# Moving the S4 weight sum of nine units by 192 bytes in a fused fp32 two-block kernel

## The reference, cut to what matters

```python
def swiglu_ffn(x, w_in, w_out):                      # first block, twice
    gate, up = jnp.split(x @ w_in, 2, axis=-1)       # 1024 x 5632
    return (jax.nn.silu(gate) * up) @ w_out

def conv_ffn(x, w_up, conv_w, conv_b, w_down):       # second block, twice
    up = x @ w_up                                    # 1024 x 5632
    a, g = up[..., :D_FF_2], up[..., D_FF_2:]
    g = causal_dwconv(g, conv_w) + conv_b
    return (jax.nn.gelu(g) * a) @ w_down

def mixer_c(x, w_in, conv_w, w_out):                 # second block, once
    proj = x @ w_in                                  # 1024 x 3072
    gate_b, gate_c, h = jnp.split(proj, 3, axis=-1)
    y = gate_b * causal_dwconv(gate_c * h, conv_w)
    return y @ w_out
```

## Time and profile before

| what | value |
|---|---|
| three timed executions | 2286.74, 2280.14, 2286.81 us; median 2286.74 |
| the profiled execution, its own time | 2293.73 us |
| its span in the trace | 2291.9 us |
| TensorE (PE) busy | 2274.3 us, 99% of the span, 15278 matmuls |
| weight loads (PEld) busy | 2081.8 us |
| VectorE, ScalarE, POOL busy | 1542.2, 1019.2, 354.9 us |
| HBM read | 234.46 MB, 103 GB/s over the span |
| mean granted clock of TensorE | 0.998 of full speed |

### The profile page before, as it was taken

One profiled execution on the slowest core, in us unless ns is written; L12 is line 12 of the kernel. 1 busy time (PEld: TensorE's weight loads), 2 busy tenths in 40 slices (PEclk: granted clock), 3 DMA queues, 4 the chain that ended last, 5 costly groups with the idle time before them and its releaser, 6 DMA issues.

```text
span 2291.9 us, 35530 instructions
## 1 busy us (share of the span) xinstructions
PE 2274.3 (99%) x15278; PEld 2081.8 (91%) x15278; DVE 1542.2 (67%) x1756; ACT 1019.2 (44%) x1283; POOL 354.9 (15%) x222
## 2 busy tenths in 40 slices
PE   9999999999999999999999999999999999999998
PEld 8999889897799998898988999988998988999987
DVE  7777436564587764356846999835886656999835
ACT  5555335455555543234333555522453442555521
POOL 2332000230133220001000322100230000322100
PEclk9999999999999999999999999999999999999999
DMA  4333323212133332242421333332233522232331
GB/s 171 111 111 111 110 74 139 74 52 78 37 113 109 111 111 102 74 173 90 168 90 37 129 105 112 112 115 77 108 100 124 200 74 74 93 108 99 129 109 55
DMA packets 34732, 238.83 MB, mean 104 GB/s; under 512 B 4108, under 2 KB 4492, under 8 KB 6800
## 3 DMA queue, kind: packets, MB, share of 16 engines
q1 hardware_dynamic: 34432, 236.56, 29.5%
q10 hardware_dynamic: 144, 0.00, 0.0%
HBM read 234.46 MB, written 2.10 MB: 103 GB/s over the span
## 4 chain that ended last, share of the span: by engine, by line
PE 96%; DVE 2%; DMA 1%; POOL 0%; ACT 0%; issue 0%; SPq 0%; DVEq 0%; POOLq 0%
PE bank L646 33%; PE bank L780 30%; PE bank L629 18%; PE bank L745 4%; PE bank L1132 4%; PE bank L768 1%; PE bank L986 1%; PE bank L1160 1%; PE bank L1181 1%; DVE w_lo L1871 1%; DMA raw<-w_full 1%; PE bank L918 0%; PE bank L928 0%; PE bank L825 0%; DVE s_lo L1987 0%
## 5 line engine op out<-in xcount | busy, mean ns | idle before, releaser
L1871 DVE TENSOR_TENSOR w_lo<-raw,w_hi 128x2048 fp32r<-128x2048 f32 (+1 forms) x207 | 475.1, 2296 | 362.5 <-ACT w_hi L1306 313.2
L1306 ACT ACTIVATE w_hi<-raw 128x2048 fp32r<-128x2048 f32 x207 | 395.1, 1909 | 326.0 <-DMA raw<-w_full 319.5
L780 PE MATMUL bank<-w_hi,h_hi 128*128 128x512 f32 x692 | 269.9, 390 | 0.0
L780 PE MATMUL bank<-w_hi,h_lo 128*128 128x512 f32 x692 | 269.4, 389 | 0.0
L780 PE MATMUL bank<-w_lo,h_hi 128*128 128x512 f32 x692 | 269.3, 389 | 0.0
L562 POOL TENSOR_TENSOR s_raw<-raw 128x512 f32<-128x512 f32 x84 | 115.7, 1378 | 545.0 <-PE bank L646 385.4
L646 PE MATMUL bank<-t_hi,s_hi 128*128 128x256 f32 x672 | 187.5, 279 | 3.2 <-ACT cc L1360 3.2
L646 PE MATMUL bank<-t_hi,w_hi 128*128 128x256 f32 x672 | 187.3, 279 | 3.0 <-DVE h L2023 3.0
L646 PE MATMUL bank<-u_hi,w_hi 128*128 128x256 f32 x672 | 187.5, 279 | 0.0
L646 PE MATMUL bank<-u_hi,w_lo 128*128 128x256 f32 x672 | 187.3, 279 | 0.0
L646 PE MATMUL bank<-u_lo,w_hi 128*128 128x256 f32 x672 | 187.2, 279 | 0.0
(11 more groups left out here) (386 smaller groups left out, 6096.9 us busy)
## 6 DMA issues: line engine op xcount, KB each, us to landing
raw<-w_full SPq DMA_DIRECT2D x207, 1024.0 KB, 4.9
rows_ab<-rows SPq DMA_DIRECT2D x8, 1024.0 KB, 7.0
x<-x SPq DMA_DIRECT2D x4, 512.0 KB, 4.5
mem_raw<-mem SPq DMA_DIRECT2D x2, 1024.0 KB, 9.0
out<-x SPq DMA_DIRECT2D x3, 512.0 KB, 2.6
raw<-w_full SPq DMA_DIRECT2D x2, 512.0 KB, 7.3
ab_rows<-ab_rows SPq DMA_DIRECT2D x1, 768.0 KB, 6.4
wg_raw<-w_gates SPq DMA_DIRECT2D x1, 512.0 KB, 7.2
```

What stands on the lines that cost most here:

```text
L780: done = mm(bank[:, 2 * t + n, :], act_in[:, k, tok(t)], w[:, s, c0:c0 + T], start=(first and r == 0 and j == 0), stop=(last and r == 1 an ...
L1306: S.activation(w_hi[:, u % SLOTS, :], raw[:, u % SLOTS, :], ACT.Copy).then_inc(w_hi_done, 1)
L1871: V.tensor_tensor(w_lo[:, u % SLOTS, at:FULL], raw[:, u % SLOTS, at:FULL], w_hi[:, u % SLOTS, at:FULL], ALU.subtract).then_inc(w_split, 1)
```

## The change

S4 gets three areas in place of two. Units with an even number take `even`, those with an odd number `odd`, both at place 0 as before; of the odd ones, the units whose distance from the run's first unit, halved and rounded down, leaves 2 when divided by 4 take `aligned`: raw and low parts at 100.6875 KB and the high part at 102.6875 KB, that is place 192, where B22 (the second 256 columns of the second half of `u`) stands. These are units 8 and 16 of runs 1 and 3, units 7 and 15 of runs 2 and 5, and unit 8 of run 4 (cin). `even` has its high part at 105 KB. Every engine's instructions stay the same in number, kind, shape and order; only addresses differ. In the changed file the lines below L130 stand 6 to 8 further down.

```diff
--- before.py
+++ after.py
@@ -126,9 +126,9 @@
         s23_raw = arena("s23_raw", [P, 2, 2 * QS], f32, 82.5)
         s23_lo = arena("s23_lo", [P, 2, 2 * QS], f32r, 82.5)
         s23_hi = arena("s23_hi", [P, 2, 2 * QS], f32r, 90.5)
-        s4_raw = arena("s4_raw", [P, 2, QS], f32, 98.5)
-        s4_lo = arena("s4_lo", [P, 2, QS], f32r, 98.5)
-        s4_hi = arena("s4_hi", [P, 2, QS], f32r, 102.5)
+        s4_place = {"even": (98.5, 105), "odd": (100.5, 102.5), "aligned": (100.6875, 102.6875)}
+        s4_whole, s4_low, s4_high = ({k: arena(f"s4_{n}_{k}", [P, QS], dt, at[i]) for k, at in s4_place.items()}
+                                     for n, dt, i in (("raw", f32, 0), ("lo", f32r, 0), ("hi", f32r, 1)))
 
         h_hi = arena("h_hi", [P, 2 * SLOTS, T], f32r, 50.5)
         h_lo = arena("h_lo", [P, 2 * SLOTS, T], f32r, 66.5)
@@ -376,6 +376,12 @@
         def lower_late(f, u):
 
             return ch_late[:, u % 2, :] if f == "c" else h32[:, u, 256:512]
+
+        def s4_kind(f, u):
+
+            if NTH_SEVEN[f, u] % 2 == 0:
+                return "even"
+            return "aligned" if (u - FIRST[f]) // 2 % 4 == 2 else "odd"
 
         def first_of_run(f, u):
             return not is_seven(f, u - 1)
@@ -554,7 +560,7 @@
             def rest_weight_sums(f, u):
 
                 j, w = NTH_SEVEN[f, u], raw[:, (U0[NAME[f]] + u) % SLOTS, :]
-                s2, s4 = s23_raw[:, j % 2, 0:QS], s4_raw[:, j % 2, :]
+                s2, s4 = s23_raw[:, j % 2, 0:QS], s4_whole[s4_kind(f, u)][:, :]
                 gp.wait_ge(first_sum, j + 1)
                 at = list(SEVENS[f]).index(u)
                 if at >= 2:
@@ -666,7 +672,7 @@
                 j, s, b = NTH_SEVEN[f, u], (U0[name] + u) % SLOTS, up_bank(f, u)
                 w = w_hi[:, s, :], w_lo[:, s, :]
                 s23 = s23_hi[:, j % 2, :], s23_lo[:, j % 2, :]
-                s4 = s4_hi[:, j % 2, :], s4_lo[:, j % 2, :]
+                s4 = s4_high[s4_kind(f, u)][:, :], s4_low[s4_kind(f, u)][:, :]
                 run_starts = first_of_run(f, u)
 
                 if split_twice(U0[name] + u):
@@ -1341,7 +1347,8 @@
                 act.wait_ge(rest_sums, j + 1)
                 act.wait_ge(third_sum, j + 1)
                 S.activation(s23_hi[:, j % 2, :], s23_raw[:, j % 2, :], ACT.Copy)
-                S.activation(s4_hi[:, j % 2, :], s4_raw[:, j % 2, :], ACT.Copy).then_inc(s_high, 1)
+                kind = s4_kind(f, u)
+                S.activation(s4_high[kind][:, :], s4_whole[kind][:, :], ACT.Copy).then_inc(s_high, 1)
 
             def copy_a11b11(f, u):
 
@@ -1985,7 +1992,8 @@
                 j = NTH_SEVEN[f, u]
                 dve.wait_ge(s_high, j + 1)
                 V.tensor_tensor(s23_lo[:, j % 2, :], s23_raw[:, j % 2, :], s23_hi[:, j % 2, :], ALU.subtract)
-                V.tensor_tensor(s4_lo[:, j % 2, :], s4_raw[:, j % 2, :], s4_hi[:, j % 2, :],
+                kind = s4_kind(f, u)
+                V.tensor_tensor(s4_low[kind][:, :], s4_whole[kind][:, :], s4_high[kind][:, :],
                                 ALU.subtract).then_inc(s_split, 1)
 
             def low_tokens(f, ks):
```

## The result

The changed kernel takes **2302.33 us** (median of four executions, 2300.31 to 2305.08), the kernel before, beside it on the same chip, 2283.44 (2279.96 to 2286.81). The ratio on record is 1.0067, with a 95% interval of 1.0042 to 1.0092 (the two medians alone give 1.0083): slower, by more than the 0.3% that can be told from no change, where I had forecast a time within 0.3%. The third case, "the S4 products leave the long pace behind them", had said 2302. Executions of one kernel differ here, in the profiles kept, because the runs can pick another pace in each; the four of the changed kernel lie 4.8 us apart from end to end, those of before 6.9.

A forecast was written before the change was run, and what follows sets the result against it. TensorE, busy 99% of the span, was taken as the bound through its start-to-start distance. Median 2286.74 - 5.2 (one run's long pace broken) + (108 - 24) x 4.4 ns = 2281.9, stated as 2282.0 us; range 2279 to 2302.5.

The forecast's parts named there:

- The third case: Rival: products after S4, from A12 B21 on, keep the long pace; 2302 us (2296 to 2305), chance 0.22.
- What bounds the kernel, and the two paces: TensorE's matmul starts set the time; distances of 113.4 (short) or 117.8 ns (long), picked at a step, then held.
- Engines other than TensorE at 0: POOL's second sum, ScalarE's copy and VectorE's subtraction write S4 in the same shapes; no wait added, cost 0.
- What the 108 matmuls cost: Nine S4 products with both operands at one place: taken at the long pace, 108 x 4.4 ns = 0.5 us.
- What they do to the pace after them: S4 products at one place break the long pace; later products go on short, 5.2 us gained in each of two runs.
- "The pace isn't touched.": Rival: the change only moves data; the median plus 0.5 us, 2287, spread 2280 to 2294; chance 0.27.
- "The loads clash.": Rival: at one place, reads of load and matmul don't overlap; up to 20.5 us, 2302, or 2292 at half; chance 0.06.
- The chances: Forecast 0.45, no effect 0.27, long pace left behind 0.22, clash 0.06; faster 0.12, same 0.65, slower 0.23.

The follow-up runs named there:

- run 3: Not a follow-up: the third of five runs inside one execution of a kernel; 1584 matmuls, 181.30 us in the profiled execution of the kernel before.
- run 4: Not a follow-up: the fourth of five runs inside one execution; the change alters only its unit 8; no time of its own is given.
- kernel 2: The changed kernel with only the first changed unit of each run (7 or 8) having S4 at B22's place: 2302.24 us, ratio 1.0071.
- kernel 1: The changed kernel with the third S4 area kept but moved to place 0, 192 bytes from B22: 2285.03 us, ratio 0.9997.
- kernel 8: The kernel before with tokens u and sums T moved 64 bytes, so every product has both operands at one place: 2321.34 us, one execution.
- kernels 1, 5: The changed kernel with its nine S4 at place 0 (2285.03 us, ratio 0.9997) and at 128 (2281.84 us, ratio 0.9975).
- kernels 5 to 7: The changed kernel with its nine S4 at 128 (2281.84 us), at 64 (2282.0), or S4 at 128 in early odd-numbered units only (2281.83).
- kernels 8 and 9: The kernel before with all products at one place (2321.34 us), and with S4 of all 84 units at 128 (2281.36 us, ratio 0.9927).

## Why the prediction was wrong

*What bounds the kernel, and the two paces.* Right. TensorE's starts set the time, 113.4 and 117.8 ns are the two paces, and a pace once set holds for long: one product in a run can set it to the run's end (runs 1 and 2 of kernel 2).

*Engines other than TensorE at 0.* Right. The waits on the products' line come to 5.7 us after and 6.2 before, and the third area alone changes nothing (kernel 1).

*What the 108 matmuls cost.* Mis-sized, with no weight: forecast 4.4 ns each over the short pace, 0.5 us; measured 120.0 - 113.4 = 6.6, 0.7 us.

*What they do to the pace after them.* This is the step that failed: "A stream at one place thus loses the long pace by itself. I therefore forecast that the S4 products at one place break the long pace, and that the products after them go on at the short one." Both sentences carried a 512-column reading over to 256 columns. The down projections with both operands at one place do run at 113.4 ns per 256 columns; but a 256-column stream at one place runs at 120.0 (kernel 8), and what follows it goes on at 117.8 (all profiles with S4 at 192). So the two runs that should have gained 5.2 us each gained nothing there, and runs 1 and 3 lost. Even behind the down projections, 512 columns at one place, products of 256 columns are not at the short pace, as the next paragraph shows. Why the two shapes differ is argued and not shown: a load's record of some 190 ns is shorter than the 226.8 ns between starts of 512 columns, but longer than the 113.4 between starts of 256, so that only there would a load lie over more than one matmul's start. I had written that difference down, and as an argument against the rival, though it speaks as much against taking the 512-column rows for my own step.

*The row that knew.* The earlier trace rows have 256 columns, 192 bytes apart, right behind a stream at one place, and all five such products took 118 ns, behind run 1 at the short pace too. They were not alone: the trace of before has more crossings of this kind, which the prediction hadn't read. After the down projection of run 3, L629 makes 48 plain matmuls of 256 columns (weights at 0, tokens at 192); the last of the projection, then the first and the last of the 48:

```profile
1604.71 0.39 PE L780 MATMUL bank<-w_hi,h_lo 128*128 128x512 f32 x1
1604.94 0.28 PE L629 MATMUL bank<-u_hi,w_hi 128*128 128x256 f32 x1
1610.47 0.28 PE L629 MATMUL bank<-u_lo,w_hi 128*128 128x256 f32 x1
```

That is 5.53 us / 47 = 117.7 ns, the long pace. The third case read the earlier trace rows as they stood: decided at A12 B21, 21.9 us on the fastest execution, 2302. It came out at 2302.33. The terms under that sum do not each agree as closely: run 3 of the profiled execution had the long pace already ahead of its S4, and run 4 lost it at a pause; these two go in opposite directions. The mechanism is right; that the sum came out within 1 us is in part luck.

*"The pace isn't touched."* Wrong too. It had leaned on the Trainium skill, "TensorE: Matmul & The Clock Gate", section "Step-by-step: what each phase is for": loading the next weights takes nothing from the running matmul's reads. By that rule, as the prediction took it, kernels 1, 5 and the change, which differ in the addresses of three arrays alone, would take the same time; they take 2285.03, 2281.84 and 2302.33 us, with ratios of 0.9997, 0.9975 and 1.0067 to the kernel before. The measurement decides here: the place matters. Whether the reads themselves take from each other no run shows.

*"The loads clash."* A small cost at one place is there: a matmul starts 6.6 ns later than at the short pace, where the far bound was 190. That this is a clash of loads isn't shown. As the cause of the 19 us between the medians it is excluded: 108 matmuls at 6.6 ns are 0.7 us, and twelve of them in a run are enough for all of the loss (kernel 2).

*The chances.* The measured 2302.33 lies inside the stated range, but only at its edge, and only because the range had been drawn up to 2302.5 for the third case, which had 0.22; the forecast with 0.45 said 2282.0, and the other way. Rows of the very crossing in question, even five of them, should have weighed more than a stream of another shape.

## What to carry to other kernels

Where TensorE is busy all the time, read start-to-start distances run by run: a spread between executions of one kernel may be two paces, and the operands' places, not the instructions, may choose between them. A few matmuls can set the pace of thousands behind them, so it can be worth finding a place that resets it (here 64 or 128 in place of 0, some 5.5 us or 0.25% below the median of the kernel before in kernels 5 to 7, and a narrower spread). And where a trace holds both a long steady stream of another shape and a short crossing of the same shape, price the change by the crossing.

## What the runs showed of the hardware that was not expected

Three distances for one form of matmul (128x256, loads beside it) at a granted clock of 1.00: 113.4, 117.8 and 120.0 ns. Which one holds depends on the distance of the loaded from the moving operand within 256 bytes, and on what ran before: 192 bytes between them (weights at 0, tokens at 192) can run at 113.4 or 117.8 and mostly keeps what it has, though a pause can change it (run 5 before, at S2 T2 of unit 7); 0 gives 120.0 and leaves 117.8; 64 or 128 bytes from loaded to moving (S4 at 128 or 64, or 256 more) leave 113.4. In the traces of both kernels and of kernels 8 and 9 the lead of a load's start over its matmul's start moves along, 110 ns at the short pace, 114 to 115 at the long one, and 117 to 118 at one place. That fits two streams of reads that keep the phase which they once fell into, but no run shows the reads themselves: why the period is 256 bytes, and why the way back from 120.0 ends at 117.8, stays open. Whether fewer than twelve matmuls would do wasn't tried.
